# A hybrid decoder layer on one core: row sums by VectorE, an early bias table, and sample states in other steps

## What is computed

```python
h = modulate(rmsnorm(x), shift1, scale1)
gq, gk, gv, gr, glr, aq, ak, av, ga, gb = split(h @ w_in)
# branch A: gated linear attention, 4 heads, dk 128, dv 256, chunks of 64
#   S = S * exp(b_last) + (k * exp(b_last - b))^T v ;  o = masked(q e^b, k e^-b) v + (q e^b) S
#   for a sample: S_new = S * exp(g) + k^T v, o = q S_new (the state is read from and written to memory)
# branch B: dilated window attention, 3 groups of 8 heads, 64 per head
s = einsum(q, k) * 64**-0.5 + bias[bucket(distance)]      # masked with -inf
p = exp(s - max(s)); den = sum(p); o = p @ v / den        # groups joined by their denominators
x = x + gate1 * ((sigmoid(ga) * y_a + sigmoid(gb) * y_b) @ w_out)
x = x + gate2 * conv_ffn(modulate(rmsnorm(x), shift2, scale2))
```

## Time and profile before

| | |
|---|---|
| median of 3 runs (lowest, highest) | 1313.89 us (1311.42, 1314.56) |
| the profiled execution | 1316.87 us, its span 1315.2 us |
| busy: TensorE, weight loads, VectorE, ScalarE, GpSimd | 93%, 87%, 46%, 35%, 8% |
| mean granted clock of TensorE | 0.96 |
| linear attention phase | from about 180 to 388 us |
| attention groups 0, 1, 2 | from about 389, 562 and 657 us |
| the small bias matmuls (L1389, L1392) | 395.6 to 399.2 us |
| the transposes of the new token (L1457) | 1.47 us |

### The profile page before, as it was taken

One profiled execution on the slowest core, in us unless ns is written; L12 is line 12 of the kernel. 1 busy time (PEld: TensorE's weight loads), 2 busy tenths in 40 slices (PEclk: granted clock), 3 DMA queues, 4 the chain that ended last, 5 costly groups with the idle time before them and its releaser, 6 DMA issues. The chain is left out here.

```text
span 1315.2 us, 23304 instructions
## 1 busy us (share of the span) xinstructions
PE 1219.5 (93%) x9759; PEld 1148.6 (87%) x9759; DVE 606.5 (46%) x972; ACT 466.7 (35%) x756; POOL 100.3 (8%) x180
## 2 busy tenths in 40 slices
PE   5899998879988999999989889998999999999997
PEld 4779997769987899899888679996999999999997
DVE  3522224553531343436537546646656655643332
ACT  3273333443341444245235244423333333322222
POOL 0000011100001000120131012000000000000000
PEclk8889998899988999999989879998999999999999
DMA  9645466544216321451444458661687888346671
GB/s 298 190 157 161 154 198 237 183 138 133 69 56 226 114 92 47 137 179 33 142 149 157 140 203 286 204 186 33 193 277 258 276 274 283 90 149 230 216 243 69
DMA packets 164225, 225.53 MB, mean 171 GB/s; under 512 B 7172, under 2 KB 147838, under 8 KB 162716
## 3 DMA queue, kind: packets, MB, share of 16 engines
q1 hardware_dynamic: 148864, 125.85, 31.3%
q10 hardware_dynamic: 1684, 54.56, 11.4%
q0 software_dynamic: 13600, 44.01, 9.9%
HBM read 200.81 MB, written 78.10 MB: 212 GB/s over the span
## 5 line engine op out<-in xcount | busy, mean ns | idle before, releaser
L376 PE MATMUL ps<-actH,whi 128*128 128x260 f32 x2064 | 442.2, 296 | 11.5 <-DVE actL L623 4.0
L376 PE MATMUL ps<-actL,whi 128*128 128x260 f32 x2064 | 421.7, 286 | 0.0
L376 PE MATMUL ps<-actH,wlo 128*128 128x260 f32 x2064 | 421.6, 286 | 0.0
L376 PEld LDWEIGHTS ps<-actH,whi 128*128 128x128 f32 x2064 | 325.6, 193 | 34.2 <-issue 28.8
L376 PEld LDWEIGHTS ps<-actL,whi 128*128 128x128 f32 x2064 | 325.3, 193 | 0.0
L376 PEld LDWEIGHTS ps<-actH,wlo 128*128 128x128 f32 x2064 | 324.8, 192 | 0.0
L360 DVE TENSOR_TENSOR wlo<-wraw,whi 128x2048 fp32r<-128x2048 f32 (+2 forms) x95 | 141.2, 1498 | 203.2 <-ACT whi L347 202.7
L347 ACT ACTIVATE whi<-wraw 128x2048 fp32r<-128x2048 f32 (+2 forms) x95 | 119.4, 1275 | 123.5 <-PE ps L376 94.3
L429 ACT ACTIVATE arena<-ps 128x520 f32<-128x520 f32 x74 | 44.5, 601 | 233.3 <-PE ps L376 233.2
L376 PE MATMUL ps<-gH,whi 128*128 128x260 f32 x352 | 71.7, 285 | 0.0
L376 PE MATMUL ps<-gL,whi 128*128 128x260 f32 x352 | 71.4, 284 | 0.0
(11 more groups left out here) (336 smaller groups left out, 1427.7 us busy)
## 6 DMA issues: line engine op xcount, KB each, us to landing
wraw<-in_w_in SPq DMA_DIRECT2D x38, 1024.0 KB, 5.3
out_win_s<-in_cache_win ACTq DMA_DIRECT2D x16, 2046.0 KB
wraw<-in_w_up SPq DMA_DIRECT2D x44, 512.0 KB, 5.9
out_win_s<-in_cache_win ACTq DMA_DIRECT2D x8, 2044.0 KB
arena<-in_w_ada SPq DMA_DIRECT2D x12, 1024.0 KB, 12.2
wraw<-in_w_ada SPq DMA_DIRECT2D x12, 1024.0 KB, 5.3
raw_gates<-arena SPq DMA_DIRECT2D x24, 260.0 KB, 5.1
arena<-raw_gates POOLq DMA_DIRECT2D x24, 260.0 KB, 4.8
```

The source lines that it names most:

```text
L376: last = pe.matmul(ps[:, 2 * (n % 2) + a, 0:HT], wt, X[:, k0 + j, a * HT:a * HT + HT], start=begin and j == 0 and wt is hi and X is H, sto ...
```

## The change

The row sums of the probabilities: the exponentials lose `accum_out`, and `settle` on VectorE does one `tensor_reduce` with add for the step before. The bias: its small matmuls move to steps 5 to 9 of `gla_in`; POOL writes the rows and the sample bias to memory there, copies every row 128 times in memory at the start of the linear attention, and loads `biasT` and `sbias` straight from it at the start of group 0, with no flips. Group 0 has 32 steps now. The sample states are updated and read in other steps, with five value buffers and a list of read steps of its own. POOL's queue is in another order, and it stores the output of the linear attention head by head.

```diff
-        VA, VB, VC = (at(c, GH * GDV) for c in (17616, 16576, 15536))
-        vwide = [VA, VB, VC, VA, VB, VA, VB, VA]
-        V_FREE = [0, 0, 0, 1, 2, 4, 5, 6]
-        O_FREE = [0, 3, 7, 8]
-        S_STEP = [3, 6, 8, 10, 13, 15, 17, 20]
-        S_FIRST, S_LAST = (0, 1, 4, 7), (0, 3, 6, 7)
+        V0, V1, V2, V3, V4 = (at(c, GH * GDV) for c in (4160, 5200, 15536, 16576, 17616))
+        vwide = [V0, V1, V2, V3, V4, V3, V4, V4]
+        V_FREE = [0, 0, 0, 0, 0, 4, 5, 7]
+        O_FREE = [0, 3, 6, 8]
+        S_STEP, R_STEP = [6, 10, 12, 13, 17, 19, 20, 24], [7, 11, 14, 14, 18, 21, 21, 25]
+        S_FIRST, S_LAST = (0, 2, 5), (None, 1, 4, 7)
...
             def read_out(step):
-                if step - 1 in S_STEP:
-                    b = S_STEP.index(step - 1)
+                for b in range(NS):
+                    if R_STEP[b] != step:
+                        continue
                     pe.wait_ge(s("gs_new"), b + 1)
...
+                elif 6 <= p < 6 + NG:
+                    g = p - 6
+                    if g == 0:
+                        pe.wait_ge(s("g_ready"), 5)
+                        pe.wait_ge(s("relb_ready"), 1)
+                    if g >= 2:
+                        pe.wait_ge(s("bvec_ready"), g - 1)
+                    pe.matmul(ps[0:AH, 4 + p % 2, 0:BW], relb[:, AH * g:AH * g + AH], onehot[:, BW * g:BW * g + BW],
+                              start=True, stop=True).then_inc(s("bvec_T"), 1)
...
+                pool.wait_ge(s("z_ready"), 1)
+                pool.dma_start(relb[0:32, :], w["rel_bias"]).then_inc(s("late_in"), 16)
+                pool.dma_start(onehot, con["onehot"]).then_inc(s("late_in"), 16)
+                pool.wait_ge(s("bvec_ready"), NG)
+                pool.dma_start(bd.rearrange("(g h) n -> h g n", g=NG), bvec).then_inc(s("bias_spilled"), 16)
+                pool.wait_ge(s("sbias"), 1)
+                pool.dma_start(sd, sbiasW.rearrange("p g n -> p (g n)")).then_inc(s("bias_spilled"), 16)
...
                 load_values(1)
+                pool.wait_ge(s("bias_spilled"), 32)
+                for lo, hi, n in ((0, AH, BW), (AH, NG * AH, 2 * P)):
+                    pool.dma_start(rd[lo:hi, :, 0:n], bd[lo:hi, 0:n].unsqueeze(1).to_broadcast([hi - lo, P, n]))\
+                        .then_inc(s("bias_spilled"), 16)
+                store_prompt(0)
                 load_state(2)
                 load_values(2)
+                store_state(0)
+                spill_out(0)
                 load_state(3)
...
                 load_state(6)
-                store_prompt(1)
                 store_state(4)
                 load_values(6)
                 load_state(7)
+                store_prompt(2)
                 store_state(5)
+                store_state(6)
                 load_values(7)
...
+        def bias_pool(pool):
+            pool.wait_ge(s("bias_spilled"), 64)
+            pool.wait_ge(s("o_spilled"), 16 * (GH + 1))
             for g in range(NG):
                 lo, hi = BC[g]
-                src = bass.AP(bd.tensor, g * AH * BW, [[1, P], [BW, AH], [1, hi - lo]])
-                sp.dma_start(hank[:, :, lo:hi], src).then_inc(s("hank_in"), 16)
+                src = bass.AP(rd.tensor, g * AH * P * BW + P - 1, [[BW - 1, P], [P * BW, AH], [1, hi - lo]])
+                pool.dma_start(biasT[:, :, lo:hi], src).then_inc(s("bias_in"), 16)
...
-                for h in range(AH):
-                    flip_pe(pe, h)
-                    yield
-                pe.wait_ge(s("bias_ready"), AH)
+                pe.wait_ge(s("bias_in"), 16 * (NG + 1))
...
+            def row_sum(j):
+
+                if j < 0:
+                    return
+                c, hs, keys = st[j]
+                n, nh = J0[g] + j, AH // 4 if g == 0 else AH // 2
+                J = P * len(keys)
+                sv = sq_[:, n % 2, 0:nh * J].rearrange("p (h k) -> p h k", k=J)
+                dve.wait_ge(s("p_ready"), n + 1)
+                dve.tensor_reduce(own(g, c)[:, AH + hs.start:AH + hs.stop:2], sv, AX.X, ALU.add).then_inc(s("row_sum"), 1)
+
             def settle(j):
+                row_sum(j - 1)
...
                 if n >= 2:
                     dve.wait_ge(s("p_T"), n - 1)
+                    dve.wait_ge(s("row_sum"), n - 1)
...
-                        last = act.activation(sv, sv, ACT.Exp, bias=own(g, c)[:, h:h + 1],
-                                              accum_out=own(g, c)[:, AH + h:AH + h + 1])
+                        last = act.activation(sv, sv, ACT.Exp, bias=own(g, c)[:, h:h + 1])
...
-                    stream_sp(sp, us[:1])
-                    if g == 0:
-                        sp.wait_ge(s("o_all"), 1)
-                        sp.dma_start(od, oT2.rearrange("p k t -> p (k t)")).then_inc(s("o_spilled"), 16)
-                    stream_sp(sp, us[1:])
+                    stream_sp(sp, us)
```

More of the change, by code:

```diff
@@ L424, in copy_tiles @@
                     to = dst[:, m0 + m, :]
-                if x.get("phase") == "gla" and x["kind"] in ("ak0", "av0") and m == 0:
-                    half = 2 * (x["kind"] == "av0") + x["m0"] % 4 // 2
-                    act.wait_ge(s(f"stored{half}"), 32)
-                    act.wait_ge(s("gs_read"), half + 5)
+                if x["kind"] == "aq0" and m == 0:
+                    act.wait_ge(s("gs_new"), 1 + x["m0"] // 2)
+                if x["kind"] in ("ak0", "av0") and m == 0:
+                    slot = 2 * (x["kind"] == "av0") + x["m0"] % 4 // 2
+                    act.wait_ge(s(f"stored{slot}"), 32)
+                    act.wait_ge(s("gs_read"), slot + 5)
                 act.activation(halves(to), banks(n), ACT.Copy).then_inc(tile_read["act"], 1)
@@ L921, in gla_in_pe @@
                     last.then_inc(s("z_ready"), 1)
+                elif 6 <= p < 6 + NG:
[7 more added lines that the diff above has]
+                              start=True, stop=True).then_inc(s("bvec_T"), 1)
+                elif p == 6 + NG:
+                    pe.wait_ge(s("bvec_ready"), 2)
+                    for g in range(NG):
+                        for i in range(g, NG + 1 if g == NG - 1 else g + 1):
+                            last = pe.matmul(ps[0:NS * AH, 5, SK * g:SK * g + SK], relbS[:, i, :],
+                                             onehot[:, NG * BW + SK * i:NG * BW + SK * i + SK], start=i == g,
+                                             stop=i == (NG if g == NG - 1 else g))
+                    last.then_inc(s("sbias_T"), 1)
                 elif p >= V_LAG and p % 2 == V_LAG % 2:
@@ L1462, in heads_tok_act @@
             for c in range(4):
-                if g == 0 and c == 2:
-                    yield
                 act.wait_ge(s("av_T"), 4 * g + c + 1)
@@ L1500, in heads_tok_dve @@
             if g == 0:
-                for h in range(FLIP_GAP + AH):
-                    yield
-                dve.wait_ge(s("flipped"), AH)
                 dve.tensor_scalar(qhl, cst[Q0:Q2, 0:AG], 0.0, None, ALU.mult)
@@ L1516, in attention_steps @@
         def attention_steps(g):
-            return 4 + len(KOUT[g]) + 1 + (1 + FLIP_GAP + AH if g == 0 else 0) + len(steps(g)) + 2 + NSS[g]
+            return 4 + len(KOUT[g]) + 1 + len(steps(g)) + 2 + NSS[g]
         def heads_tok_sp(sp, g):
@@ L1655, in attend_dve @@
             yield
-            settle(len(st) + 1)
+            for at_step, what, c, n in due:
+                what(c, n)
             yield
@@ L1760, in attention_pool @@
             if g == 0:
[L1761 removed]
+                bias_pool(pool)
             heads_tok_sp(pool, g)
```

124 lines of the change are left out of this document (44 added, 80 removed).

## The result

| | before | after |
|---|---|---|
| median of the runs, us | 1313.88 | 1276.57 |
| lowest to highest, us | 1311.42 to 1314.56 | 1274.05 to 1278.76 |
| profiled execution, us | 1316.87 | 1278.76 |
| its span, us | 1315.2 | 1277.1 |
| mean granted clock | 0.960 | 0.968 |

The ratio is 0.972, with a 95% interval of 0.970 to 0.974: the change takes 37.3 us off the median, and 38.1 us off the profiled execution, where the sum of the prediction had 43.2 (42.2 with its allowance). The forecast was 1272, the time is 4.6 us above it.

What follows compares the result with a forecast made beforehand. TensorE, busy 93%, sets the end with its work, idle waits and half clock. Terms -24.2 (sample states), -16.5 (bias table) and -2.5 (row sums) sum to -43.2 us: 1270.7 against the median, with 1 us allowance 1272, range 1264 to 1279.

Steps and rivals of the forecast that it cites:

- its allowance: Whole kernel: 1 us allowed for small waits, since margins of 0.1 to 1.3 us came from one execution.
- Sample states, waits and clock: Linear attention: three long TensorE waits (5.29, 5.07, 7.08 us) and 6.8 us of half clock go; -24.2 us.
- The margin of 1.3 us: Linear attention, step 10: update ready at about 245.1, TensorE reads at about 246.4, so no wait.
- The two side remarks: Linear attention: state recursion still waits twice about 1 us; sample 6's late values hold ScalarE 3 to 5 us, bound 0 to +3.
- Sample 4 has that position now; I keep it: Linear attention: the fourth wait, 0.6 us, a read behind a weight split at a unit's start, stays.
- The bias matmuls in the projection phase: Moved there from group 0: their own time cancels, and they bring a wait of +0.3 us, bounds 0 and +1.
- L919 ends at 95.9, two places on is 101.7: Projection phase: TensorE's arrival at step 6; a place is 24 matmuls, 2.9 us at full clock.
- Bias table and flips: Attention group 0: flips 6.9, table wait 5.0, its half clock 2.25, earlier query step 2.7 us gained.
- Row sums: Attention: dropping accumulator reads of 0.10 us from ScalarE's exponentials gives -2.5 us, bounds -3.5 and 0.
- the alternative in the prediction: Attention exponentials: by the skill's 0.41 us without accumulator, removing it is worth nothing and the sum 2.5 us smaller.
- Priced at 0, bounds 0 and +6: Attention: 32 added row sums, about 19 us of VectorE, fit its idle time; +6 if a third on the path.
- Row copies crowd the transfers: Rival, linear attention: 3.7 MB of copies delay a weight load or gate store 11 us, 2.6 of clock; 1286, chance 0.05.

Runs made afterwards that it cites:

- e2: The changed kernel with sample states back in the old steps, old three value buffers and POOL's old order; 1295.4 us, ratio 0.989.
- the second profile: The changed kernel run again unchanged, as yardstick beside the follow-up runs; 1276.0 us, ratio 0.973.
- e5: The changed kernel with sample 4 read in step 21 with samples 5 and 6 instead of step 18; 1267.5 us, ratio 0.968.
- e1: The changed kernel with row sums put back into the exponentials as accumulators, none on VectorE; 1278.8 us, ratio 0.975.
- e7: The changed kernel with every row sum computed twice on VectorE; ratio 0.976, 4.3 us slower than the changed kernel.
- e9: The changed kernel with both bias row copies issued a second time to memory nobody reads; ratio 0.977, 5.4 us slower than the changed kernel.
- e8: The changed kernel with row sums over only the first 8 keys, so its result is wrong; 1275.9 us, ratio 0.971.

## Why the prediction was right, and where its terms were off

**Sample states, waits and clock: right.** -17.4 and -6.8 were forecast. The three long waits and their half clock are gone from both profiles of the changed kernel and come back with the old steps, with nearly the same lengths (e2). Undoing cost 19.4 us with the row sums on VectorE and 24.4 with the accumulators; the linear attention of the ledger has 22.9 and 23.8. The margin of 1.3 us at the read of sample 1 was right: the update ends at 242.6 and TensorE reads at 244.0. The two side remarks held as well. The state recursion waits twice for 1.1 us, as before. ScalarE's wait for the values of sample 6 is 4.8 us (3.4 in the second profile) where 3 to 5 were said, and TensorE pays nothing for it:

```profile
297.79 1.71 ACT L1086 ACTIVATE arena<-arena 128x256 f32<-128x256 f32 x4 [4.79 <-DMA arena<-sample_values]
```

**Sample 4's wait: mis-sized.** "Sample 4 has that position now; I keep it" took 0.6 us from another sample. It is 2.5 us, in four of seven profiles with half clock in addition; e5 puts it at 3.5. The prediction counted the weight split ahead of the update, but not what stands ahead of the split. VectorE and ScalarE around it, after:

```profile
281.59 1.70 ACT L1086 ACTIVATE arena<-arena 128x256 f32<-128x256 f32 x4
283.19 0.59 ACT L433 ACTIVATE arena<-ps 128x520 f32<-128x520 f32 x1
283.67 1.91 ACT L349 ACTIVATE whi<-wraw 128x2048 fp32r<-128x2048 f32 x1
...
285.61 2.29 DVE L362 TENSOR_TENSOR wlo<-wraw,whi 128x2048 fp32r<-128x2048 f32 x1 [1.79 <-ACT whi L349]
287.82 1.67 DVE L1136 SCALAR_TENSOR_TENSOR arena<-arena 128x256 f32<-128x256 f32 x4
```

ScalarE scales the values of this very sample first, for 1.7 us, then copies a tile and only then makes its half of the split. VectorE, done with the head's gates at 283.8, stands 1.8 us and then has the split before the update.

**The bias matmuls in the projection phase: the step that failed.** It was forecast that their own time cancels and that the wait is 0.3 us. The own time does cancel (3.7 us here, 3.6 in group 0 before). The wait is 3.3 us with 2.7 us of half clock behind it, six instead of 0.3. The wrong step is "L919 ends at 95.9, two places on is 101.7". VectorE's side was right to 0.1 us, if one takes off the 0.6 by which the trace is early. But TensorE reached 95.9 that late only because this execution had lost 3 us to half clock at 87 to 93 us. I had not read the clock of the phase from which I took the time of arrival. e1, e7 and e9 show it: the same code with that half clock waits 0.2 us. Where the stretch stays away, 3 us come back as a gain that nobody forecast, so that the phase lost 5.5 to 6.5 us against before instead of 4. As far as these profiles show, that gain is luck and no part of the change. How often the kernel before has the stretch is not known, since there is one trace of it.

**Bias table and flips: right.** Group 0 was forecast at 6.9 + 5.0 + 2.25 + 2.7 and 3.6 us of bias matmuls taken out, 20.5 us; it gained 20.5 to 20.9 in every kernel run. Some of that agreement is chance: a wait of TensorE for its own sequencer (PEq) at the end of the group was 2.20 us before and 1.10 to 1.13 after, which was not forecast, so the other terms together are 1 us short. The query parts were said to be in time to 0.1 us; they are 0.28 us late, where the wait was 2.87:

```profile
395.83 0.71 PE L1543 MATMUL ps<-arena 64*128 64x128 f32 x8 [0.28 <-DVE query_parts L1503]
```

The table was in time in all kernels. The medians of its loads were 7.5 to 9.7 us, inside the 10.1 that the prediction allowed. The load of the samples' bias behind them, which TensorE waits for with them, took 10.0 to 11.5; in the first profile it had landed at 385.7, and TensorE asked at 395.5.

**Row sums: right in the mechanism, near in size.** Forecast 2.5 us for the accumulator reads and nothing for VectorE's sums, shown 3.0 in the waits, 0.2 for the first sum, and 2.8 for both in the ledger. Four exponentials of 128 columns now take 1.19 us up to ScalarE's next instruction, 0.30 each, against 0.41 with the read the earlier trace rows:

```profile
547.85 1.28 ACT L1678 ACTIVATE arena<-arena 128x128 f32<-128x128 f32 x4 [3.49 <-DVE arena L1651]
549.04 0.61 ACT L349 ACTIVATE whi<-wraw 128x512 fp32r<-128x512 f32 x1
```

The Trainium skill ("ScalarE: Activation LUTs", section "Rules for kernel authors") has 0.41 us without an accumulator, an estimate from its budget. The trace agrees if that is the duration of one ACTIVATE: it is 0.39 to 0.40 in the earlier trace rows. What counts here is the distance of two that follow each other, and that is 0.30 without the read. So the alternative in the prediction, by which the removal is worth nothing, took a duration for a distance; going by the trace gave the right sign. "Priced at 0, bounds 0 and +6" holds with 0.2 for one sum a step and 3 to 4 for two (e7, e8).

**Row copies crowd the transfers: did not decide, and nearly did.** The rival's chain exists (4.2 and 8.2 us of ScalarE's waiting), and it reaches TensorE at some point between one and two sets of copies (e9). 0.05 was small for a margin that size; "a unit's weights are asked for over a unit ahead" was the wrong cover to check. It held: the weight loads of this stretch landed in 7.4 us before, 13.2 after and 26.5 in e9 (medians), and ScalarE's longest wait for one of them stayed at 5.7 to 5.9. What reached TensorE were the stores whose buffers ScalarE fills. The rule of the Trainium skill on the number of engines of a DMA ("DMA: Bandwidth & Descriptors", section "Rules for kernel authors") is not settled by any run here. The copy of 8 rows was not slower per byte than the one of 16 issued behind it (1.5 MB in 18.5 us, 2 MB in 26.8).

**The sum.** By stage the forecast of 43.2 is -3.9 for the projection phase, 24.2, 20.5, and 2.5 for the row sums. The ledger of the first profile has -6.5, 23.5, 20.8 and 2.1, together 40.0: the projection phase misses by 2.6 (the wait and its half clock cost 5.7 more, the half clock that stayed away gave 2.9 back), and in the linear attention only 0.7 of the 1.9 for sample 4 are to be seen. Outside these stages 0.6 were gained ahead of them and 2.5 lost behind the attention, where nothing was changed; that leaves the 38.1 measured. In the second profile the stage behind gains 1.4, and the span is 1274.3.

## What to carry to other kernels

A time of arrival read from one execution contains that execution's half-clock stretches: before a margin of a few us is drawn from it, read the granted clock of the phase in which the arrival was earned. Where a task stands behind a weight split, count the whole queue of the engine that feeds the split, not only the split. That an added operation is hidden says nothing of the next one: here the first row sum cost 0.2 us and the second 3.2. To find how much room is left, double what seems to be hidden, an operation or a transfer, and measure.

## What the runs showed of the hardware

- Short waits are followed by half clock in some executions and not in others, at the same place of the same code. At L924 (L914 before) TensorE waits twice for 1.0 to 1.5 us, 5 us apart. Behind the second wait five of fourteen profiles went to 0.50 for 5 to 7 us, and behind the first three others for 3.4 us; those three don't wait a second time. Behind 2.5 us at L1012 four of seven did. Each costs 1.7 to 3 us of work, and shifts what TensorE waits for next.
- A copy of 1.5 MB in DRAM that repeats rows, issued beside full traffic, landed after 18.5 us, one of 2 MB after 26.8; with a second set beside them after 22.0 and 32.7. DMAs of another queue land later beside them (medians before, after, with the second set): stores of 260 KB 6.3, 8.4 and 17.3 us, weight loads of 1 MB 7.4, 13.2 and 26.5.
- An accumulator read adds 0.10 us to an exponential of 128 columns on ScalarE, a quarter of its pitch.
